# Attention with the output projection inside its loop, and a reordered stick-breaking mixer

## The chip, the cores and the metric

One core of a Trainium2 chip runs the whole program. Its engines each take their own instructions in order and meet at semaphores: TensorE (PE; PEld is its weight load), VectorE (DVE), ScalarE (ACT), GpSimd (POOL) and SyncE (SP, which issues DMAs). PSUM, where matmuls write, has 8 banks of 512 float32 values for each of 128 partitions. The metric is the device time of one execution in microseconds (us).

## What is computed

256 tokens of width 1024 pass a first block of two layers (feed-forward, mixer, feed-forward, gated embedding) and a second block of two layers (attention, then experts chosen by a top-k). The three places that matter here, cut down:

```python
# first block, layer 0: stick-breaking attention, 16 heads of 64
q, k, v = jnp.split(h @ w_qkv, 3, axis=-1)
q = rms_norm(q.reshape(B, S, 16, 64), q_gain)      # and k alike
z = jnp.einsum('bhqd,bhkd->bhqk', qb, kb) * scale
log_stay = jnp.where(causal, jax.nn.log_sigmoid(-z), 0.0)
log_after = lax.cumsum(log_stay, axis=3, reverse=True) - log_stay
weights = jnp.where(causal, jnp.exp(jax.nn.log_sigmoid(z) + log_after), 0.0)
o = einsum('bhqk,bhkd->bhqd', weights, vb);  return o @ w_o

# second block, layer 0 (MLA, keys of 128 + 64 rotated) and layer 1 (DSA), 8 heads of 128
s = einsum(q, k) * scale;  s = jnp.where(mask, s, -jnp.inf)
p = jax.nn.softmax(s, axis=-1);  o = einsum(p, v);  return o @ w_o
# in DSA the mask is a top-64 of an index score for each query
```

## The kernel before, in words

All weights come as a stream of units of 128 x 1024 float32 (512 KB). SP loads them into a ring of 6 (`raw`). `split` makes two parts of a unit: ScalarE copies it to a rounded high part (`w_hi`, ring of 4, line 655) and VectorE subtracts that to get the low part (`w_lo`, ring of 6, line 1106). ScalarE may split unit u only when unit u-4 is used. TensorE waits for the low part in `unit()` and multiplies with three matmuls per product (`mm3`, lines 1848 to 1850): high by high, high by low, low by high. `rows` multiplies the 256 tokens by 8 units into `acc(0)` (banks 0 to 3) or `acc(1)` (banks 4 to 7): 12 matmuls of 512 columns a unit.

The order on each engine is the order written in its function, and each function calls `split` at chosen places, so the place of a `split` in ScalarE's and VectorE's lists is fixed. Of the loops, only the feed-forward one is a loop on the chip; all others are written out.

**Stick-breaking mixer** (layer 0 of the first block). TensorE: q's rows into acc(0), k's into acc(1); it waits for the copy of k, transposes q (`turn_rows`, line 1880) into banks 0 to 3, multiplies v into acc(1), and behind v's sixth unit waits for k's normed rows and transposes k into banks 0 to 3. `head_norm` on VectorE squares (line 1234), reduces, waits for GpSimd's power (line 488) and multiplies (line 1242), with splits between. `keep_acc` on ScalarE (line 728) copies a product out of PSUM; `keep_turned` (line 714) copies transposes. Then `stick_breaking`: for 8 pairs of heads, TensorE's logits (lines 1982, 1983), VectorE's mask and size (1267, 1269), ScalarE's exp and log (791, 792), VectorE's stay (1274), TensorE's sums (1991, 1992), ScalarE's exp (782), TensorE's mix (2000 to 2002), ScalarE's high and VectorE's low part of the output (786, 1279). A pair uses two banks, in turn over all 8. The output projection goes into acc(0), and `late_norm` transposes x into banks 4 to 7.

**Attention** (MLA and DSA), 8 heads. A head's scores (TensorE, line 2032) go to bank n % 4; VectorE masks them (1328 in MLA, two instructions; 1331 in DSA, one) and takes the maximum (1336); ScalarE's exp (818); VectorE divides by the sum (1342, 1344); TensorE transposes the weights (2047) into bank 4 or 5; ScalarE copies them (824); TensorE mixes (2057, 2058) into bank 6 or 7; ScalarE takes the high part (810) and VectorE the low part (1248) of the head's output. Turn n of VectorE handles the mask of head n, the division of n-1 and the low part of n-3; turn n of ScalarE the exp of n, the copy of n-1 and the high part of n-2. There is no split within the loop: up to four units of the projection are split ahead of it, the rest behind. When all heads are done, `rows` runs the projection: 8 units into acc(0), and the layer norm follows. In DSA VectorE finds the top 64 in 8 rounds ahead of the attention, each with a split ahead of it, and TensorE transposes q (banks 0 to 3) and k (banks 4 to 7) behind v's rows.

Of the kernel before, what the change touches and what calls it, by code (L numbers as in the profile page):

```python
# [24 lines left out]
F32 = mybir.dt.float32  # L25
# [34 lines left out]
KEY_TURN = 5  # L60
# [47 lines left out]
KEPT_MLA = 3 + PARTS + 2  # L108
N_UNITS = sum(n for _, n in unit_plan()) + SPLIT
# [110 lines left out]
def program(nc, stream, x_in_dram, consts, stickc, poolc, scalec, ropec, lnc, subkeys, out):  # L220
    with ExitStack() as ctx:
# [166 lines left out]
        def logit(p):  # L388

            r = 2 * (p % 4)  # L390
            return ps[:, r:r + 2, 0:PAIR]

        def mixed(p):
            r = 2 * (p % 4)
            return ps[:, r:r + 2, PAIR:PAIR + P]
# [26 lines left out]
        diags, row = blk(E_DIAG, DIAG_RING, NK), blk(E_ROWS, ROW_RING, 2 * D)  # L422

# [214 lines left out]
        def _(act):  # L638
# [139 lines left out]
            def stick_breaking():  # L778
# [29 lines left out]
            def heads_high(k, bank):  # L808
                act.wait_ge(o_done, t.after(o_done))
                act.activation(act_hi[:, k, :], ps[:, bank, 0:T], ACT.Copy).then_inc(o_hi, 1)  # L810
# [92 lines left out]
            for i in range(DEPTH):  # L903
# [3 lines left out]
                if i == 0:  # L907
# [27 lines left out]
                early_norm(4 * i + 2, 1 + i)  # L935
# [11 lines left out]
            for i in range(DEPTH):  # L947
# [5 lines left out]
                if i == 0:  # L953
# [50 lines left out]
                    attention(M_SM, M_PT)  # L1004
                else:
# [25 lines left out]
                    split(KD)  # L1031
                    keep_acc(v_tok, 1)
                    keep_turned(area(A_QT, 2048), range(4))
                    keep_turned(area(A_KT, 2048), range(4, 8))
                    attention(S_SM, S_PT)
                if i == 1:
                    split(KD - SPLIT)
# [7 lines left out]
                split(KD - 1)  # L1045
# [45 lines left out]
        def _(dve):  # L1091
# [136 lines left out]
            def head_norm(rows, scale, eps):  # L1228
# [15 lines left out]
                split(KD - 5)  # L1244

            def heads_low(k, bank):
                dve.wait_ge(o_hi, t.after(o_hi))
                dve.tensor_tensor(act_lo[:, k, :], ps[:, bank, 0:T], act_hi[:, k, :].bitcast(F32),
# [12 lines left out]
            def stick_breaking():  # L1261
# [30 lines left out]
                for p in range(2, N_PAIRS):  # L1292
# [3 lines left out]
                    if p + 2 < N_PAIRS:  # L1296
                        stays(p + 2)
                output_low(N_PAIRS - 1)
# [21 lines left out]
            def attention(sm_at, mask, scale):  # L1320
                sm = blk(sm_at, H2, PAIR)
                parts = ((0, P), (P, PAIR))
                for n in range(H2 + 3):
                    if n < H2:
                        dve.wait_ge(s_done, t.after(s_done))
                        if isinstance(scale, list):
                            for b, (lo, hi) in enumerate(parts):
                                ins = dve.scalar_tensor_tensor(sm[:, n, lo:hi], ps[:, n % 4, lo:hi], scale[b],
                                                               mask[:, lo:hi], ALU.mult, ALU.add)
                        else:  # L1330
                            ins = dve.scalar_tensor_tensor(sm[:, n, :], ps[:, n % 4, 0:PAIR], scale, mask,
# [15 lines left out]
                    if n >= 3:  # L1347
                        heads_low(n - 3, 6 + (n - 3) % 2)
# [39 lines left out]
            for i in range(DEPTH):  # L1388
# [3 lines left out]
                if i == 0:  # L1392
# [3 lines left out]
                    head_norm(q_tok, 1.0, HD * EPS)  # L1396
                    head_norm(k_tok, 1.0 / HD, EPS)
# [3 lines left out]
                    for n in range(PARTS):  # L1401
                        b, c = part(n, 1)
                        dve.tensor_tensor(x[:, b, c], acc(0)[:, b, c], x[:, b, c], ALU.add).then_inc(x_ready, 1)
# [9 lines left out]
                early_norm(4 * i + 2, 1 + i)  # L1413
# [9 lines left out]
            for i in range(DEPTH):  # L1423
# [7 lines left out]
                if i == 0:  # L1431
# [40 lines left out]
                    attention(M_SM, area(M_ROPE + 128, PAIR), [small[:, 22 + b:23 + b] for b in range(TB)])  # L1472
# [1057 lines left out]
```

## Time and profile before

| | us |
|---|---|
| median of 3 runs (lowest, highest) | 2760.16 (2758.28, 2761.77) |
| the profiled execution | 2757.85 |
| its span | 2756.0 |
| TensorE busy / VectorE / ScalarE / GpSimd | 2542.8 / 2062.0 / 1279.2 / 1147.6 |
| stick-breaking mixer, q's rows to the end of its projection | 205 to 338 |
| MLA attention and its projection | 1062.6 to 1112.7 |
| DSA attention and its projection | 2024.9 to 2067.6 |
| last stage (rows gathered for the experts) | 2067.7 to 2756 |

Times of the trace count from the span's start. A row of a timeline has its start, its length, the engine, the line of the kernel, the operation, what it writes and reads, and how many like it follow one another; in brackets stands how long the engine was idle before it and whose work it waited for. `arena` is the big tile in SBUF in which nearly everything lives, `ps` is PSUM, `act_both` holds the high and low parts of the activations. The length of an instruction includes a part in which the next one already runs, so the distance of two starts is what an instruction takes in a row of such.

### The profile page before, as it was taken

The page shows a single profiled execution, that of the slowest core. Times are in us where ns is not written, and L with a number is a line of the kernel's source. Part 1 is how long each engine was busy: PE and PEld are TensorE (multiplying, and loading weights), DVE is VectorE, ACT ScalarE, POOL GpSimd, SP SyncE. Part 2 cuts the span into 40 slices and gives each one's busy share as a digit, 9 for nine tenths or more (in the row PEclk, how much of TensorE's full clock was granted, in tenths as well). Part 3 has the DMA queues.
Part 4 walks back from the last instruction along what each step waited for, and adds up shares of the span by engine and source line. Part 5 has one row for each costly group of instructions (what it writes and reads, how often), then busy time and mean ns, then how long its engine had stood idle before and what let it go on. Part 6 is the DMA issues. An engine that isn't in the chain of part 4 may idle for free.

```text
span 2756.0 us, 38867 instructions
## 1 busy us (share of the span) xinstructions
PE 2542.8 (92%) x12724; PEld 1980.0 (72%) x12724; DVE 2062.0 (75%) x4122; ACT 1279.2 (46%) x2160; POOL 1147.6 (42%) x1482
## 2 busy tenths in 40 slices
PE   8999899999999999999999899999987888887777
PEld 7887688878888877899999788887765333433223
DVE  7886588788878876798999567666777776777675
ACT  5555555555555555555555445455443222222222
POOL 4443044344434411388787533331103444444443
PEclk9999999999999999999999999999999999999998
DMA  9996799889979966455556799997938999999998
GB/s 356 379 320 211 283 384 373 279 328 377 324 264 383 368 222 218 153 175 182 183 180 198 250 382 389 383 385 285 314 129 341 422 416 422 412 422 419 414 411 341
DMA packets 217832, 873.30 MB, mean 317 GB/s; under 512 B 38320, under 2 KB 38448, under 8 KB 184048
## 3 DMA queue, kind: packets, MB, share of 16 engines
q0 software_dynamic: 118496, 511.47, 47.6%
q1 hardware_dynamic: 99072, 359.38, 37.0%
q10 hardware_dynamic: 144, 1.05, 0.1%
q8 instruction: 51, 0.84, 0.1%
q14 instruction: 69, 0.57, 0.1%
HBM read 786.70 MB, written 152.17 MB: 341 GB/s over the span
## 4 chain that ended last, share of the span: by engine, by line
PE 50%; DMA 21%; POOL 12%; DVE 7%; issue 5%; ACT 3%; SPq 0%; DVEq 0%; POOLq 0%; ACTq 0%
PE ps L1931 12%; DMA arena<-both_rows,arena 11%; POOL gate_cells L544 11%; PE ps L1848 8%; PE ps L1849 8%; PE ps L1850 8%; DMA both_rows<-in_stream 8%; PE ps L2294 6%; PE ps L1933 6%; DVE arena L1739 2%; PE ps L2251 1%; DMA raw<-in_stream 1%; DVE w_lo L1106 1%; PE ps L2032 1%; ACT w_hi L655 1%
## 5 line engine op out<-in xcount | busy, mean ns | idle before, releaser
L1106 DVE TENSOR_TENSOR w_lo<-raw,w_hi 128x1024 fp32r<-128x1024 f32 x665 | 811.0, 1223 | 290.4 <-ACT w_hi L655 285.8
L655 ACT ACTIVATE w_hi<-raw 128x1024 fp32r<-128x1024 f32 x665 | 701.8, 1058 | 461.0 <-DMA raw<-in_stream 316.3
L2294 PE MATMUL ps<-arena 128*128 128x512 f32 x1024 | 483.1, 620 | 126.5 <-ACT arena L872 126.4
L1931 PE MATMUL ps<-act_both,w_hi 128*128 128x512 f32 x1408 | 502.3, 399 | 6.6 <-DVE act_both L1134 4.8
L2294 PEld LDWEIGHTS ps<-arena 128*128 128x128 f32 x1024 | 192.8, 196 | 406.1 <-ACT arena L872 204.4
L1739 DVE SCALAR_TENSOR_TENSOR arena<-arena 128x1024 f32<-128x1024 f32 x256 | 313.6, 1225 | 186.6 <-DMA arena<-both_rows,arena 184.9
L583 POOL DMA_INDIRECT arena<-both_rows,arena x256 | 290.5, 1135 | 369.5 <-PE ps L2294 342.5
L516 POOL DMA_DIRECT2D both_rows<-arena x512 | 280.1, 554 | 353.1 <-DVE arena L1183 343.4
L1848 PE MATMUL ps<-w_hi,act_both 128*128 128x512 f32 (+1 forms) x990 | 386.0, 390 | 26.1 <-DVE w_lo L1106 12.8
L1933 PE MATMUL ps<-act_both,w_lo 128*128 128x256 f32 x1408 | 394.8, 280 | 0.0
L1849 PE MATMUL ps<-w_lo,act_both 128*128 128x512 f32 (+1 forms) x990 | 383.0, 387 | 0.0
L1850 PE MATMUL ps<-w_hi,act_both 128*128 128x512 f32 (+1 forms) x990 | 382.5, 387 | 0.0
L544 POOL DMA_INDIRECT gate_cells<-hot x256 | 316.0, 1235 | 110.2 <-issue 83.2
L1848 PE MATMUL ps<-act_both,w_hi 128*128 128x256 f32 x1192 | 339.5, 285 | 3.6 <-DVE act_both L1140 1.5
L1849 PE MATMUL ps<-act_both,w_hi 128*128 128x256 f32 x1192 | 338.0, 284 | 0.0
L1850 PE MATMUL ps<-act_both,w_lo 128*128 128x256 f32 x1192 | 337.9, 283 | 0.0
L1931 PEld LDWEIGHTS ps<-act_both,w_hi 128*128 128x128 f32 x1408 | 264.5, 188 | 74.9 <-issue 4.5
L1933 PEld LDWEIGHTS ps<-act_both,w_lo 128*128 128x128 f32 x1408 | 265.8, 189 | 3.0
L865 ACT ACTIVATE hot<-hot 128x2 f32<-128x2 f32 (+1 forms) x132 | 26.8, 203 | 458.3 <-DVE arena L1739 457.5
L1848 PEld LDWEIGHTS ps<-w_hi,act_both 128*128 128x128 f32 x990 | 188.1, 190 | 69.6 <-DVE w_lo L1106 12.0
L1848 PEld LDWEIGHTS ps<-act_both,w_hi 128*128 128x128 f32 x1192 | 229.4, 192 | 5.1 <-issue 3.8
L1849 PEld LDWEIGHTS ps<-act_both,w_hi 128*128 128x128 f32 x1192 | 229.5, 193 | 0.0
(276 smaller groups left out, 3652.8 us busy)
## 6 DMA issues: line engine op xcount, KB each, us to landing
raw<-in_stream SPq DMA_DIRECT2D x675, 512.0 KB, 3.4
arena<-in_stream POOLq DMA_DIRECT2D x128, 512.0 KB, 9.7
both_rows<-arena POOLq DMA_DIRECT2D x512, 128.0 KB, 6.3
both_rows<-in_stream POOLq DMA_DIRECT2D x128, 512.0 KB, 7.0
gate_cells<-hot POOLq DMA_DIRECT2D x32, 512.0 KB, 21.2
hot<-gate_cells POOLq DMA_DIRECT2D x128, 128.0 KB, 7.0
gate_cells<-hot POOLq DMA_INDIRECT x256
arena<-both_rows,arena POOLq DMA_INDIRECT x256, 10.8
```

What stands on the lines that cost most here:

```text
L516: pool.dma_start(rows.rearrange("(c r) k -> r c k", r=32), arena[32 * a:32 * a + 32, A_RELAY_OUT + UNIT * s:A_RELAY_OUT + UNIT * s + UNIT] ...
L544: pool.indirect_dma_start(gate_cells[:, :], bass.IndirectOffsetOnAxis(ap=cell[:, q:q + 1], axis=0), weights[:, q:q + 1], None).then_inc(sc ...
L583: pool.indirect_dma_start(row[:, p % ROW_RING, :], None, both_rows[:, :], at).then_inc(row_in[p % ROW_RING], 16)
L655: act.activation(w_hi[:, u % SPLIT, :], raw[:, u % RAW, :], ACT.Copy).then_inc(hi_done, 1)
L1106: dve.tensor_tensor(w_lo[:, u % RAW, :], raw[:, u % RAW, :], w_hi[:, u % SPLIT, :].bitcast(F32), ALU.subtract).then_inc(lo_done, 1)
L1739: dve.scalar_tensor_tensor(row[:, p % ROW_RING, 0:D], row[:, p % ROW_RING, 0:D], 1.0, x_rows[:, b, :], ALU.mult, ALU.mult, accum_out=dots[ ...
L1848: pe.matmul(dst, lhs[0], rhs[0], start=first, stop=False, **kw)
L1849: pe.matmul(dst, lhs[0], rhs[1], start=False, stop=False, **kw)
L1850: return pe.matmul(dst, lhs[1], rhs[0], start=False, stop=last, **kw)
L1931: pe.matmul(ps[:, bank, :], high, act_both[:, :, k, :], start=k == 0, stop=k == KD - 1, skip_group_check=True)
L1933: ins = pe.matmul(ps[:, bank, T:2 * T], low, act_hi[:, k, :], start=False, stop=k == KD - 1, skip_group_check=True)
L2294: ins = pe.matmul(ps[:, 2 * (n % 2) + half, :], diags[:, p % DIAG_RING, :], row[:, p % ROW_RING, D + 512 * half:D + 512 * half + 512], sta ...
```

## The change

- Stick-breaking: v's rows go to acc(0), q's banks, right behind k's rows. q is transposed behind v's second unit and k behind its seventh, both into banks 4 to 7. The pairs start at banks 4 to 7, the projection goes to acc(1), and the following norm transposes into banks 0 to 3. ScalarE copies k ahead of a split instead of behind it and v ahead of two; those two splits come within the last two turns of the loop.
- Attention: banks 0 to 3 hold the first four heads' scores and then the projection's sums; later heads' scores go to banks 4 and 5. There is one bank for transposed weights (6) and one for a head's output (7). In turn n TensorE transposes the weights of head n, multiplies unit n - lag of the projection, mixes head n and makes the scores of head n + 4; lag is 2 in MLA, 3 in DSA. `mix(n)` waits for the copy of its own weights and for the low part of head n-1. ScalarE and VectorE split one unit at the end of their turns 5 to 9 (MLA) and 3 to 10 (DSA).
- DSA: q and k are transposed behind v's third and sixth unit, both into banks 0 to 3, and the top-k has a split in the first 4 of its 8 rounds.

```diff
-KEY_TURN = 5
+QUERY_TURN, KEY_TURN = 1, 6
+SCORE_BANK, WEIGHT_BANK, MIX_BANK = (0, 1, 2, 3, 4, 5, 4, 5), 6, 7
+MLA_LAG, DSA_LAG = 2, 3
+MLA_SPLITS, DSA_SPLITS = range(5, 10), range(3, 11)
...
         def logit(p):
-            r = 2 * (p % 4)
+            r = (2 * p + 4) % 8
...
 # ScalarE
+                    else:
+                        split()
                 output_high(N_PAIRS - 1)
...
-            def attention(sm_at, pt_at):
+            def attention(sm_at, pt_at, splits):
-                for n in range(H2 + 2):
+                for n in range(H2 + 3):
...
-                        act.activation(pT[:, n - 1, :], ps[:, 4 + (n - 1) % 2, 0:PAIR], ACT.Copy).then_inc(p_kept, 1)
-                    if n >= 2:
-                        heads_high(n - 2, 6 + n % 2)
+                        act.activation(pT[:, n - 1, :], ps[:, WEIGHT_BANK, 0:PAIR], ACT.Copy).then_inc(p_kept, 1)
+                    if 2 <= n < H2 + 2:
+                        heads_high(n - 2)
+                    if n in splits:
+                        split()
...
-                    split(KD)
-                    keep_acc(k_tok, 1, roots=1)
-                    keep_turned(area(A_QT, 2048), range(4), cst[:, QG:QG + 1])
-                    split(KEY_TURN + 1)
-                    keep_turned(area(A_KT, 2048), range(4), cst[:, KG:KG + 1])
+                    split(KD - 1)
+                    keep_acc(k_tok, 1, roots=1, pending=1)
+                    split(3)
+                    keep_turned(area(A_QT, 2048), range(4, 8), cst[:, QG:QG + 1])
+                    split(KD - SPLIT)
+                    keep_turned(area(A_KT, 2048), range(4, 8), cst[:, KG:KG + 1])
                     act.preload_act_table_set("natural_log_exp_and_others")
-                    split(KD - KEY_TURN - 1)
-                    keep_acc(v_tok, 1, roots=1)
+                    keep_acc(v_tok, 0, roots=1, pending=2)
...
-                    split(KD)
-                    keep_acc(v_tok, 1)
+                    split(2)
                     keep_turned(area(A_QT, 2048), range(4))
-                    keep_turned(area(A_KT, 2048), range(4, 8))
-                    attention(S_SM, S_PT)
+                    split(2)
+                    keep_turned(area(A_KT, 2048), range(4))
+                    keep_acc(v_tok, 1, pending=SPLIT)
+                    attention(S_SM, S_PT, DSA_SPLITS)
...
 # VectorE
-                split(KD - 5)
+                split(after)
...
                     if n >= 3:
-                        heads_low(n - 3, 6 + (n - 3) % 2)
+                        heads_low(n - 3)
+                    if n in splits:
+                        split()
...
-                    head_norm(q_tok, 1.0, HD * EPS)
-                    head_norm(k_tok, 1.0 / HD, EPS)
+                    head_norm(q_tok, 1.0, HD * EPS, KD - 6)
+                    head_norm(k_tok, 1.0 / HD, EPS, 2)
...
-                        if n < KD:
+                        if n < KD - SPLIT:
                             split()
...
 # TensorE
-            def attention(sm_at, pt_at, terms, values_pending=False):
+            def attention(sm_at, pt_at, terms, lag):
+                used, ready = t.value(s_used), t.value(act_ready)
                 def scores(h):
-                    if h >= 4:
-                        pe.wait_ge(s_used, t.after(s_used))
-                    s, both = ps[:, h % 4, :], terms(h)
+                    if h >= 6:
+                        pe.wait_ge(s_used, used + h - 1)
+                    s, both = ps[:, SCORE_BANK[h], :], terms(h)
...
+                def turn_weights(h):
+                    pe.wait_ge(p_ready, t.after(p_ready))
...
+                def mix(h):
+                    pe.wait_ge(p_kept, t.after(p_kept))
+                    if h >= 1:
+                        pe.wait_ge(act_ready, ready + h)
...
+                def project(h):
+                    if h == 0:
+                        pe.wait_ge(s_used, used + 4)
+                    pe.wait_ge(act_ready, ready + h + 1)
+                    s = unit()
+                    for b in range(TB):
+                        for lo in (0, 512):
+                            ins = mm3(ps[:, 2 * b + lo // 512, :], a(h, P * b, P), w(s, lo, 512), h == 0, h == H2 - 1)
...
+                for n in range(H2 + lag):
+                    if n < H2:
+                        turn_weights(n)
+                    if n >= lag:
+                        project(n - lag)
+                    if n < H2:
+                        mix(n)
+                        if n + 4 < H2:
+                            scores(n + 4)
...
-                    rows(1, KD, fresh=False, then={KEY_TURN: turn_keys})
+                    rows(0, KD, fresh=False, then={QUERY_TURN: turn_queries, KEY_TURN: turn_keys})
                     stick_breaking()
-                    rows(0, KD, fresh=False, by_part=part_done, late=(KD - 2, KD - 1))
+                    rows(1, KD, fresh=False, by_part=part_done, late=(KD - 2, KD - 1))
...
+                    rows(1, KD, fresh=False, then={2: turn_q, 5: turn_k})
+                    pe.wait_ge(turned_kept, t.after(turned_kept, 4))
+                    attention(S_SM, S_PT, lambda h: ((kT[:, h, :], qT[:, h, :]),), DSA_LAG)
```

## Rows read from the trace of the kernel before

**Rows 1.** The page, part 1: TensorE's busy time, share of the span, instructions.
```profile
PE 2542.8 (92%) x12724; PEld 1980.0 (72%) x12724; DVE 2062.0 (75%) x4122; ACT 1279.2 (46%) x2160; POOL 1147.6 (42%) x1482
```
**Rows 2.** Busy time by stretch: us, busy (instructions) of each engine, clock, DMA.
```profile
1112.70:1125.00 12.30, 6.41 (x27) 5.72 (x28) 6.90 (x21) 8.58 (x16) 1.82 (x3) 0.63 0.37 130
2024.80:2045.70 20.90, 15.24 (x89) 11.89 (x89) 18.32 (x63) 15.49 (x50) 0.55 (x1) 1.00 0.00 0
```
**Rows 3.** Timeline of TensorE, stick-breaking: start, length, instruction, [idle before, releaser].
```profile
247.11 1.91 PE L1880 MATMUL ps<-cst,arena 128*128 128x128 f32 x16
250.48 0.50 PE L1848 MATMUL ps<-w_hi,act_both 128*128 128x512 f32 x1 [1.47 <-ACT arena L728]
...
269.05 3.34 PE L1880 MATMUL ps<-cst,arena 128*128 128x128 f32 x16 [1.95 <-DVE arena L1242]
...
278.06 0.71 PE L1982 MATMUL ps<-arena 64*128 64x256 f32 x4
...
285.03 0.91 PE L1991 MATMUL ps<-arena 128*128 128x384 f32 x2 [2.01 <-DVE arena L1274]
```
**Rows 4.** Timelines of GpSimd, VectorE and ScalarE in the same stage.
```profile
258.47 6.33 POOL L488 TENSOR_TENSOR small<-small,cst 128x32 f32<-128x32 f32 x1 [17.30 <-DVE small L1237]
...
266.71 2.28 DVE L1242 TENSOR_TENSOR arena<-arena,small 128x2048 f32<-128x2048 f32 x1
...
279.19 2.10 ACT L728 ACTIVATE arena<-ps,small 128x1024 f32<-128x1024 f32 x2
...
280.46 0.69 DVE L1267 TENSOR_TENSOR ps<-ps,arena 128x512 f32<-128x512 f32 x1
```
**Rows 5.** Timeline of TensorE, MLA attention and the start of its projection.
```profile
1073.26 0.55 PE L2047 MATMUL ps<-cst,arena 128*128 128x128 f32 x3
1073.64 0.60 PE L2057 MATMUL ps<-arena 128*128 128x256 f32 x2
...
1074.30 2.06 PE L2032 MATMUL ps<-arena 128*128 128x128 f32 x8
...
1086.43 0.55 PE L2047 MATMUL ps<-cst,arena 128*128 128x128 f32 x3 [1.70 <-DVE arena L1344]
...
1090.60 0.50 PE L1848 MATMUL ps<-w_hi,act_both 128*128 128x512 f32 x1 [0.93 <-DVE act_both L1248]
```
**Rows 6.** Timelines of ScalarE and VectorE: pieces of an attention turn, and splits.
```profile
1073.85 0.49 ACT L824 ACTIVATE arena<-ps 128x384 f32<-128x384 f32 x1 [1.01 <-PE ps L2047]
1074.50 0.39 ACT L810 ACTIVATE act_both<-ps 128x256 fp32r<-128x256 f32 x1 [0.16 <-PE ps L2058]
...
1090.13 0.42 DVE L1248 TENSOR_TENSOR act_both<-ps,act_both 128x256 fp32r<-128x256 f32 x1 [0.42 <-ACT act_both L810]
...
2048.80 1.06 ACT L655 ACTIVATE w_hi<-raw 128x1024 fp32r<-128x1024 f32 x1 [3.62 <-PE ps L1850]
2051.52 1.06 ACT L655 ACTIVATE w_hi<-raw 128x1024 fp32r<-128x1024 f32 x1 [1.66 <-PE ps L1850]
...
2049.90 1.23 DVE L1106 TENSOR_TENSOR w_lo<-raw,w_hi 128x1024 fp32r<-128x1024 f32 x1 [4.26 <-ACT w_hi L655]
```
**Rows 7.** Timelines of TensorE and then of VectorE, DSA attention.
```profile
2024.86 2.89 PE L2032 MATMUL ps<-arena 128*128 128x128 f32 x16 [1.94 <-ACT arena L714]
2029.50 0.55 PE L2047 MATMUL ps<-cst,arena 128*128 128x128 f32 x3 [1.76 <-DVE arena L1344]
...
2045.69 0.50 PE L1848 MATMUL ps<-w_hi,act_both 128*128 128x512 f32 x1 [0.93 <-DVE act_both L1248]
...
2023.47 1.23 DVE L1106 TENSOR_TENSOR w_lo<-raw,w_hi 128x1024 fp32r<-128x1024 f32 x1
...
2026.44 0.56 DVE L1331 SCALAR_TENSOR_TENSOR arena<-ps,arena 128x384 f32<-128x384 f32 x1
...
2027.56 0.55 DVE L1331 SCALAR_TENSOR_TENSOR arena<-ps,arena 128x384 f32<-128x384 f32 x1
...
2029.36 0.55 DVE L1331 SCALAR_TENSOR_TENSOR arena<-ps,arena 128x384 f32<-128x384 f32 x1
```

More of the change, by code:

```diff
@@ L1003, in _ @@
                     keep_acc(v_tok, 1)
-                    attention(M_SM, M_PT)
+                    attention(M_SM, M_PT, MLA_SPLITS)
                 else:
@@ L1044, in _ @@
                     continue
-                split(KD - 1)
+                split(KD - 1 - len(MLA_SPLITS))
                 layer_norm()
@@ L1226, in ffn, with head_norm @@
                                              ALU.add).then_inc(x_ready, 1)
-            def head_norm(rows, scale, eps):
+            def head_norm(rows, scale, eps, after):
                 dve.wait_ge(acc_kept, t.after(acc_kept))
@@ L1318, in heads_of, with attention @@
                 return tok(at, row)[:, :, off:off + h * d].rearrange("p b (h d) -> p b h d", h=h)
-            def attention(sm_at, mask, scale):
+            def attention(sm_at, mask, scale, splits):
                 sm = blk(sm_at, H2, PAIR)
@@ L1471, in _ @@
                     t.skip(acc_kept, 3)
-                    attention(M_SM, area(M_ROPE + 128, PAIR), [small[:, 22 + b:23 + b] for b in range(TB)])
+                    attention(M_SM, area(M_ROPE + 128, PAIR), [small[:, 22 + b:23 + b] for b in range(TB)],
+                              MLA_SPLITS)
                 else:
@@ L2036, in attention @@
                 for h in range(4):
                     scores(h)
-                if values_pending:
-                    pe.wait_ge(acc_kept, t.after(acc_kept))
-                for n in range(1, H2 + 2):
-                    if n <= H2:
-                        h = n - 1
-                        pe.wait_ge(p_ready, t.after(p_ready))
-                        if h >= 2:
-                            pe.wait_ge(p_kept, t.after(p_kept))
-                        for c in range(3):
-                            ins = pe.transpose(ps[:, 4 + h % 2, P * c:P * c + P],
-                                               sm[:, h, P * c:P * c + P], ident)
-                        ins.then_inc(p_turned, 1)
-                    if n >= 2:
-                        h = n - 2
-                        if h == 0 or h == H2 - 1:
-                            pe.wait_ge(p_kept, t.after(p_kept))
-                        if h >= 2:
-                            pe.wait_ge(act_ready, t.after(act_ready))
-                        o, v = ps[:, 6 + h % 2, :], slice(P * h, P * h + P)
-                        pe.matmul(o[:, 0:T], v_tok[:, 0, v], pT[:, h, 0:T], start=True, stop=False)
-                        pe.matmul(o[:, P:T], v_tok[:, 1, v], pT[:, h, T:PAIR], start=False,
-                                  stop=True).then_inc(o_done, 1)
-                    if n + 3 < H2:
-                        scores(n + 3)
@@ L2073, in _, with turn_queries @@
                 if i == 0:
+                    def turn_queries():
+                        pe.wait_ge(acc_kept, t.after(acc_kept))
+                        pe.wait_ge(rows_ready, t.after(rows_ready))
+                        turn_rows(q_tok, range(4, 8))
                     def turn_keys():
@@ L2076, in turn_keys @@
                         pe.wait_ge(turned_kept, t.after(turned_kept, 4))
-                        turn_rows(k_tok, range(4))
+                        turn_rows(k_tok, range(4, 8))
                     rows(0, KD)
@@ L2188, in terms @@
                         return (kT[:, h, :], qT[:, h, :]), (krT[r, :], qrT[r, h // 2, :])
-                    attention(M_SM, M_PT, terms, True)
+                    attention(M_SM, M_PT, terms, MLA_LAG)
                 else:
```

77 lines of the change are left out of this document (42 added, 35 removed).

## The prediction

> **What bounds the kernel now.** I read the page first: TensorE is busy 92% of the span [rows 1], so a change that only reorders work can win no more than the TensorE waits of the stages that it touches. The timeline of TensorE through each of the three stages then gives those waits, and the timelines of the other engines say who ends them.
>
> Stick-breaking stage: TensorE stands 1.47 us ahead of v's rows, until ScalarE has copied k out of PSUM, and 1.95 us ahead of the key transposes, until VectorE has multiplied k by its root [rows 3]. These 16 transposes then took 3.34 us where the same 16 took 1.91 us at 247.11 [rows 3]: the array had fallen to the lower of its two clocks (1.2 instead of 2.4 GHz). Then v's copy starts only at 279.19, behind a split on ScalarE, and the first size at 280.46, behind a split on VectorE [rows 4], and the first sums wait 2.01 us [rows 3]. From there the chain VectorE, ScalarE, VectorE sets the pace.
>
> MLA attention: TensorE has work almost without a pause; of the loop's waits only 1.70 us (weights of head 6) and 0.93 us ahead of the projection are worth a name [rows 5]. DSA attention: VectorE sets the pace, and in 20.9 us TensorE is busy 15.24 [rows 2]. It starts late because VectorE's top-k runs to 2026.44 [rows 7].
>
> **Stick-breaking.** q, k and v take the same matmuls. v goes to q's banks, so it needs neither k's copy nor q's transposes; both sets of transposes come behind v's units 1 and 6. I lay the stage out from the end of k's rows, 246.94 (0.17 ahead of the row at 247.11, as at any end of a run of matmuls here). TensorE's own work to the end of v is 8 units of 2.72 us (from ScalarE's starts at 2048.80 and 2051.52, each released by a unit [rows 6]) and two transposes of 1.72 (1.91 less the overlap with the next): 25.2, so 272.1, if nothing waits. Query transposes at 252.4: k's copy, with the split now behind it, is done at 249.4. Key transposes at 267.7: k's squares start at 249.4, split and reduction follow, GpSimd's root takes 6.33 us [rows 4] to 261.8, four splits lie beside it, the product of 2.28 us [rows 4] ends at 264.3. So there are 3 us to spare, and no fall of the clock. Before, the logits started at 278.06 [rows 3]: 5.9 us gained. The copy of v now starts at once and the first size at 273.1, since no split stands ahead of either; from there size, exp, log and stay are the same chain (280.46 to 285.03 before [rows 3, 4]), so the first sums come at 277.7 instead of 285.03. **Gain 7.4 us.** What is late next is the same VectorE and ScalarE chain, and it is not changed. The two splits put into its last two turns fall where ScalarE has no exp waiting; they delay the last output by about 1.2 us, and that is used only by the projection's eighth unit, 19 us later. The norm that moves to banks 0 to 3 costs nothing: it waits for the same x, and those banks are free by then.
>
> **The two attention loops.** Removed: the pass of 8 projection units behind the loop, 8 x 2.72 = 21.8 us, and the waits of 1.70 and 0.93 [rows 5] or 0.93 [rows 7]. Added: the same 8 units in the turns. Moved: 5 and 8 splits on ScalarE and VectorE. The number of matmuls is the same; the new order of the score matmuls I cost at nothing, between -1 and +1 us. Prefetch on SP follows the units, which are now used more slowly, so it has more time; GpSimd's load of the sub-keys, behind the last mix, has 6.6 us to land and is first read behind the layer norm, over 15 us later: nothing.
>
> What counts is a new wait. There is now one bank for a head's output, so the mix of head n waits until VectorE has taken the low part of head n-1. Follow what lies between two mixes, by start to start times. Low part to matmul 0.47 (1090.13 to 1090.60 [rows 5, 6]); mix 0.66 [rows 5]; scores 1.99 in MLA (2.06 less the overlap [rows 5]) or 0.73 in DSA (2.89 for four heads [rows 7]), while there are any (turns 0 to 3); transposes to ScalarE's copy 0.59 [rows 5, 6]; the copy 0.39 (0.49 less 0.10 overlap) and the high part 0.28 [rows 6]. Now comes the split, last in ScalarE's turn: high to low 1.10 and the low part of the weights 1.14 (1.23 less 0.09 overlap) [rows 6], and only behind it, in VectorE's next turn, mask, maximum and division, 1.80 together (the two masks at 2027.56 and 2029.36 [rows 7]), and then the low part of head n. Without scores that is 6.4 us, with them 7.15 in DSA; MLA's mask is two instructions, so I take 6.6 there. TensorE's own turn is 0.38 + 2.72 + 0.66 = 3.76, or 4.49 with scores. So every turn with a split in it leaves TensorE waiting 2.6 to 2.8 us: **the splits have been put into a ring that runs through all three engines.** Without a split the ring is 3.5 to 4 us, and TensorE hides it.
>
> MLA, scores from 1062.64 as before. Turns 0 and 1 have no projection to hide the one bank: waits of 0.75 and 1.48, mix 1 at 1076.2. Turns 2 and 3 are TensorE's own (0.38 + 2.72 + 0.66 + 1.99 = 5.75). The first split is in turn 5 of ScalarE, behind the transposes of head 4 (1090.4), so mix 4 waits: 1096.3; then mix 5 at 1102.9, mix 6 at 1108.2, mix 7 at 1112.8 (no mask any more), and two units to 1119.4. Before, 1090.60 + 21.8 = 1112.4 [rows 5]. **Loss 7.0 us.**
>
> DSA. q and k are transposed within v's rows, and 4 of the 8 splits leave the top-k, each 1.14 (one stands at 2023.47 [rows 7]): mask 0 at 2026.44 - 4.56 = 2021.9; TensorE has the scores from 2020.2, for which the two transposes fill a pause of 0.8. Transposes of head 0 at 2025.5 (3.06 behind the mask as before [rows 7], and 0.5 more for v's copy and the exp table on ScalarE). Mix 0 26.6, mix 1 29.9; turn 3 of VectorE holds the first split, so mix 2 waits 5.4 us, to 2037.0; then 2044.2, 2051.3, 2057.7, 2063.0, 2067.6, and three units to 2076.6. Before, 2045.69 + 21.8 = 2067.5 [rows 7]. **Loss 9.1 us**, although the loop starts 4.6 us earlier.
>
> Restarts: a first matmul behind a wait is 0.10 longer (0.50 against 0.40), some ten times: 1 us at most. The clock: it fell to 0.63 on average over 1112.7 to 1125, after 4.6 us without work, and stayed at 1.00 in the DSA loop with waits up to 1.9 [rows 2, 7]. The 5.4 us wait ahead of mix 2 is in the first class: I take 1.3 us for it, between 0 and 3. A page bears on this: the Trainium skill ("TensorE: Matmul & The Clock Gate", Why this matters for your kernels) says that a longer gap between bursts sends the array back to the half clock; by that rule each wait of 2.8 us might do it, which is the third rival below.
>
> Sum: -7.4 + 7.0 + 9.1 + 0.6 + 1.3 = +10.6 us. Everything behind each stage follows its end: the feed-forward stages have TensorE busy, and the last stage starts from the layer norm. The profiled execution took 2757.85 us (span 2756.0), so 2768.5; it lies 2.3 below the median of the runs shown. I say 2769.
>
> **Rivals.** (1) The ring doesn't bind, TensorE does: the split is done early because ScalarE reaches it before the transposes. Then DSA's loop is its own work, 36 us and 6 of first waits, from 2020.2 to 2062.2 (-5.4), MLA's ends at 1110.9 (-1.5), and with the stick-breaking gain the sum is -14.3: 2743.6. For it speaks that most of the work is TensorE's [rows 1]; against it that ScalarE takes its instructions in the order written, and the split stands behind the copy of the turned weights. It decides as soon as the ring is under 4.5 us. The Trainium skill has a rule against this change even then ("Perfetto Trace Analysis", Optimizing Tensor Performance): matmul groups should rotate through PSUM banks so that emptying one overlaps the next. By it alone, with the splits out of the way, one mix bank costs only the first two turns of a loop, 2 us each, which is in this rival's sum.
> (2) The ring is there but shorter, since less of each piece is exposed than start to start times say: losses of 3 and 4.5 us against the gain of 7.4: 2758.
> (3) The clock falls within the loops and stays low. TensorE's turn doubles from 4.49 to 9.0 in DSA and from 3.76 to 7.5 in MLA, over the ring: some 6 and 2 us more: 2777. For it: waits of 2.7 us in every turn; against it: 1.00 in rows 2 at 73% busy.
> (4) The stick-breaking part gives nothing, because the clock or the chain takes it back: 2776.
>
> **Chances.** Forecast 0.58 (own range 2762 to 2775), (1) 0.13, (2) 0.13, (3) 0.11, (4) 0.05. The range reaches over the forecast, (2) in its upper half, (3) and (4): 2756 to 2780, leaving out (1) and the tails. A measurement of this kernel can tell about 0.2%, 5.5 us, from no change: faster by more (under 2754.6) 0.14, within 0.14, slower by more (over 2765.7) 0.72.
>
> **What would show it.** Right: in the profile after, the mixes wait for VectorE's low part 2.6 to 2.8 us a turn in the second half of MLA's loop and all through DSA's, the longest ahead of mix 2 of DSA; VectorE's splits there wait 3 us for ScalarE's; from the first scores to the end of the projection MLA takes 56.8 us instead of 49.8 and DSA 56.4 instead of 42.6; the stick-breaking stage has no wait ahead of v and the key transposes. Wrong: loops in which TensorE has no waits after turn 2 (rival 1), or a granted clock of 0.5 through them (rival 3), or a stick-breaking gain under 5 us.

## The result, and the profile after

| | before | after |
|---|---|---|
| median of ten runs each, us | 2758.11 (2753.23 to 2762.13) | 2765.77 (2763.12 to 2769.97) |
| the profiled execution, us | 2757.85 | 2763.59 |
| its span, us | 2756.0 | 2761.8 |

The ratio is 1.0028, with a 95% interval of 1.0018 to 1.0037: 7.7 us slower. The forecast was 2769 us, in a range of 2756 to 2780.

The page's busy times hardly moved (after; compare [rows 1]):

```profile
PE 2541.1 (92%) x12724; PEld 1980.0 (72%) x12724; DVE 2059.4 (75%) x4122; ACT 1276.7 (46%) x2160; POOL 1147.4 (42%) x1482
```

TensorE is busy 1.7 us less (its busy time includes time at the lower clock) and the span is 5.8 us longer, so it waits 7.5 us more. The reader finds where by laying the same landmarks of the two TensorE timelines side by side. The x transposes that open each norm are good ones, since every kernel has them. The stages between them, in us:

| kernel | to the norm behind stick-breaking | from there to MLA's scores | MLA scores to norm | to the norm of the DSA block | from there to the norm behind DSA's attention | of it from DSA's scores | rest of the span |
|---|---|---|---|---|---|---|---|
| before | 338.1 | 724.5 | 54.6 | 800.8 | 152.7 | 45.9 | 685.3 |
| after | 330.0 | 721.7 | 59.4 | 800.2 | 165.1 | 64.3 | 685.4 |

Stick-breaking gave 8.1 us (0.7 of it was there at 199 us already, ahead of the stage), MLA's loop cost 4.8 (5.3 to the last matmul of its projection; the wait ahead of the norm is 0.5 shorter), DSA's stage 12.5. TensorE in the stick-breaking stage after (columns as in [rows 3]): no wait ahead of v or of the key transposes, 1.91 us instead of 3.34 for them, first sums at 276.95 instead of 285.03.

```profile
251.43 1.91 PE L1896 MATMUL ps<-cst,arena 128*128 128x128 f32 x16
...
266.81 1.91 PE L1896 MATMUL ps<-cst,arena 128*128 128x128 f32 x16
```

TensorE in MLA's loop after ([rows 5] before): L2049 scores, L2056 transposes of the weights, L2064 the mix. The mixes of heads 1 and 4 to 7 wait for VectorE's low part (L1260):

```profile
1051.68 6.77 PE L2049 MATMUL ps<-arena 128*128 128x128 f32 x32
...
1063.82 0.67 PE L2064 MATMUL ps<-arena 128*128 128x256 f32 x2 [1.41 <-DVE act_both L1260]
...
1074.67 0.59 PE L2064 MATMUL ps<-arena 128*128 128x256 f32 x2
...
1082.91 0.67 PE L2064 MATMUL ps<-arena 128*128 128x256 f32 x2 [2.69 <-DVE act_both L1260]
...
1089.99 0.67 PE L2064 MATMUL ps<-arena 128*128 128x256 f32 x2 [1.50 <-DVE act_both L1260]
```

And in DSA's loop after ([rows 7] before):

```profile
2018.58 1.02 PE L2064 MATMUL ps<-arena 128*128 128x256 f32 x2 [0.58 <-ACT arena L834]
...
2023.36 0.67 PE L2064 MATMUL ps<-arena 128*128 128x256 f32 x2 [1.41 <-DVE act_both L1260]
...
2030.49 1.19 PE L2064 MATMUL ps<-arena 128*128 128x256 f32 x2 [5.25 <-DVE act_both L1260]
...
2039.28 0.67 PE L2064 MATMUL ps<-arena 128*128 128x256 f32 x2 [1.57 <-DVE act_both L1260]
...
2046.42 1.19 PE L2064 MATMUL ps<-arena 128*128 128x256 f32 x2 [2.53 <-DVE act_both L1260]
...
2053.93 0.67 PE L2064 MATMUL ps<-arena 128*128 128x256 f32 x2 [2.03 <-DVE act_both L1260]
```

The length of a mix tells the clock: 0.67 us is full speed behind a wait, 0.59 without one, 1.0 to 1.2 the lower level. It tells it for that moment only: behind the mix of 0.67 us at 1082.91 the clock fell, and the granted clock of that turn was 0.76 on average. One turn of VectorE and ScalarE between the mixes at 2039.28 and 2046.42 shows the ring link by link:

```profile
2041.19 0.49 ACT L834 ACTIVATE arena<-ps 128x384 f32<-128x384 f32 x1 [2.03 <-PE ps L2056]
2041.58 0.38 ACT L820 ACTIVATE act_both<-ps 128x256 fp32r<-128x256 f32 x1
2041.84 1.06 ACT L663 ACTIVATE w_hi<-raw 128x1024 fp32r<-128x1024 f32 x1
...
2042.94 1.23 DVE L1118 TENSOR_TENSOR w_lo<-raw,w_hi 128x1024 fp32r<-128x1024 f32 x1 [3.81 <-ACT w_hi L663]
2044.08 0.55 DVE L1346 SCALAR_TENSOR_TENSOR arena<-ps,arena 128x384 f32<-128x384 f32 x1
...
2045.86 0.42 DVE L1260 TENSOR_TENSOR act_both<-ps,act_both 128x256 fp32r<-128x256 f32 x1
```

High part 2041.58, ScalarE's split 2041.84, VectorE's split 1.10 later (after 3.81 us of waiting for it), mask 1.14 later, low part 1.78 later, mix 0.56 later. The distance of the two mixes is 7.14 us; the prediction's ring had 7.15.

### The profile page after: what moved, and what is told of

The parts are those of the page before. It is cut to its first block, busy times and chain, and to the rows that moved or that the text cites. A ratio compares the mean times of both kernels' runs of the same rounds, so it can differ in the third digit from the quotient of the medians.

```text
span 2761.8 us, 38878 instructions
## 1 busy us (share of the span) xinstructions
PE 2541.1 (92%) x12724; PEld 1980.0 (72%) x12724; DVE 2059.4 (75%) x4122; ACT 1276.7 (46%) x2160; POOL 1147.4 (42%) x1482
## 4 chain that ended last, share of the span: by engine, by line
PE 47%; DMA 23%; POOL 12%; DVE 8%; issue 6%; ACT 3%; SPq 0%; DVEq 0%; POOLq 0%; ACTq 0%
DMA arena<-both_rows,arena 12%; PE ps L1947 12%; POOL gate_cells L552 11%; DMA both_rows<-in_stream 10%; PE ps L1864 7%; PE ps L1865 7%; PE ps L1866 7%; PE ps L1949 6%; PE ps L2328 5%; DVE arena L1755 2%; DVE w_lo L1118 1%; PE ps L2285 1%; DMA raw<-in_stream 1%; ACT w_hi L663 1%; PE ps L2049 1%
```

## The experiments

The times of the kernel before shift a little from one set of runs to the next, so each ratio is to the runs beside it. Theory throughout: two splits of one unit, placed in the same turn, tie low part n to low part n+1 through ScalarE. Rivals: the single mix bank alone; TensorE's own work; the clock.

**Stick-breaking alone.** Edit: the parts of the diff on q, k, v and the banks 0 to 3 of the next norm, on the kernel before; both attentions as before.

> The kernel before with the stick-breaking part alone; both attention loops as before. My theory: the whole gain of that part, 7.4 us, is kept to the end, so 2750.7 us against 2758.1 (ratio 0.9973), with 330.0 instead of 338.1 us at the x transposes behind the stage, and no stage behind it changed. In the changed kernel MLA's scores also came 3.1 us earlier than this gain explains (before, ScalarE's splits in MLA's preparation wait for weights to land). If that belongs to where the transfers fall once the stick-breaking stage is shorter, it shows here too: about 2748 us (0.996), scores at 1051.7. If it was chance, scores are at 1054.8. Rival: what the stage gains is given back downstream, ratio 1.000.

Measured: ratio 0.9982 (0.9973 to 0.9991), 5.0 us faster, the forecast of 7.4 at the edge of the interval. The stage itself is as in the changed kernel (norm behind it at 330.6), and the later stages are those of before: 54.6 and 45.9 us for the two attentions. MLA's scores came at 1053.42, between the two values named, which settled nothing yet (the next experiment and the last one settle it). The gain is kept to the end.

**Each loop alone beside it.** Edit: the changed kernel with the three `attention` functions, splits and bank numbers of before called for MLA (first) or for DSA with its order of transposes (second).

> The changed kernel with MLA's attention put back as before: stick-breaking part and DSA loop alone. My theory: the parts add. In the trace of the changed kernel the DSA stage ends 12.4 us later against the clock of its own start (-6.8 at 1911, +5.6 at the end of the projection), so -7.4 + 12.4 = +5.0: 2763.1 us (ratio 1.002). If the price of the DSA loop were only the 9.1 us of my prediction, +1.7: 2759.8 (1.0006). Rival: the loss came mostly from MLA's loop, then 2751 (0.997).

> The changed kernel with DSA's attention and the order of its q and k transposes put back as before: stick-breaking part and MLA loop alone. My theory: MLA's loop costs what its stage shows, from the first scores to the end of the projection 55.2 instead of 49.9 us, +5.3, beside -7.4 and the 3.1 us found ahead of the scores: -5.2, 2752.9 us (ratio 0.998). By my prediction's 7.0 for the loop and without the 3.1: -0.4, 2757.7 (1.000). Rival: an attention loop with the projection inside is no loss in itself, then 2748 (0.996).

Measured: with the DSA loop 1.0029 (1.0017 to 1.0041), with the MLA loop 1.0004 (0.9994 to 1.0014). The 1.002 expected of the first lies within its interval; the 0.998 expected of the second doesn't, and 1.000, the prediction's 7.0 without the 3.1 us ahead of the scores, does. Against stick-breaking alone that is +13 and +6 us; by the stages, DSA 164.7 against 151.9 (+12.8) and MLA 60.0 against 54.6 (+5.4). By the stages the costs add, 18.2 us where the changed kernel has 17.3. By the times of whole executions they add less well: 13 and 6 make 19, and the changed kernel lies 12.7 above stick-breaking alone (1.0028 against 0.9982), which the intervals of about 0.1% each just allow. Neither kernel lost anything in the stage that it has as before. From the norm behind stick-breaking to MLA's scores the first took 720.6 us, the second 723.3, with the same instructions up to there. All eleven kernels with the new stick-breaking stage, the changed one among them, lie between 720 and 724 us there, and the timelines of ScalarE differ in that stretch by what its splits wait for a weight unit to land (3.85 us once at 1052.05 in the kernel before; 3.38 us once at 1042.83 in the kernel with stick-breaking alone; 2.66 and 1.74 us in the kernel of the next experiment). The kernel before took 724.5 us there. The last kernel below is the kernel before with only its MLA score matmuls in another order, so its code is the same up to there, and it took 721.8, with waits of 2.30 and 1.45 us. So the 2.8 us that the changed kernel gained there are not its own.

**ScalarE's splits one turn earlier.** The smallest cut through the ring; bank, lags and VectorE stay.

```
-MLA_SPLITS, DSA_SPLITS = range(5, 10), range(3, 11)
+MLA_HIGH, DSA_HIGH = range(4, 9), range(2, 10)
+MLA_LOW, DSA_LOW = range(5, 10), range(3, 11)
```

> The changed kernel with ScalarE's splits one turn earlier in both loops and VectorE's where they are, so VectorE's split no longer waits for the high part of the next head. One mix bank, lags and all else stay. My theory: the ring is cut, since low part of head n, split, mask, division and low part of head n+1 (3.4 us) run beside low part, mix, scores, transposes, copy, high part (3.1 us). TensorE's own turn (5.4 and 3.8 us in MLA, 4.5 and 3.8 in DSA) then decides: MLA's waits ahead of mixes 4 to 6 go (-6 us at least), in DSA mix 2 waits under 2.5 us instead of 5.25 and the others under 0.5, the clock stays at 1.00: -14 us. Sum -18 to -24 against the changed kernel: 2742 to 2748 us (0.994 to 0.996 of the kernel before). Rival A: the single mix bank is the cause by itself, the split only fills a wait that is there anyway: the mixes still wait 2.6 us a turn, 2766 (1.003). Rival B: ScalarE's earlier splits wait for a unit that the projection has not freed or for its landing, and delay exp and copy: 2755 to 2760.

Measured: 0.9962 (0.9948 to 0.9976), 2744.09 us, 10.5 faster than before and some 18 faster than the changed kernel. MLA takes 52.1 us from scores to norm, 7.3 less than in the changed kernel, and DSA 47.6, 16.7 less (at least 6 and 14 were expected). The clock did not stay at 1.00 in the first turns: 0.76 granted behind mix 1 of MLA, 0.62 behind mixes 0 and 1 of DSA. TensorE's timeline, MLA and then DSA:

```profile
1062.82 0.84 PE L2065 MATMUL ps<-arena 128*128 128x256 f32 x2 [1.41 <-DVE act_both L1261]
...
1080.69 0.59 PE L2065 MATMUL ps<-arena 128*128 128x256 f32 x2
...
1084.44 0.59 PE L2065 MATMUL ps<-arena 128*128 128x256 f32 x2
...
2015.21 1.19 PE L2065 MATMUL ps<-arena 128*128 128x256 f32 x2 [1.40 <-DVE act_both L1261]
...
2020.15 0.67 PE L2065 MATMUL ps<-arena 128*128 128x256 f32 x2 [1.40 <-DVE act_both L1261]
...
2024.63 0.59 PE L2065 MATMUL ps<-arena 128*128 128x256 f32 x2
...
2029.00 0.59 PE L2065 MATMUL ps<-arena 128*128 128x256 f32 x2
```

Past mix 2 no mix waits, and their distances are TensorE's own 3.75 and 4.4 us. Within the loops VectorE's splits now wait at most 0.52 us for ScalarE's, instead of 2.4 to 5.9:

```profile
2028.20 1.23 DVE L1119 TENSOR_TENSOR w_lo<-raw,w_hi 128x1024 fp32r<-128x1024 f32 x1 [0.52 <-ACT w_hi L664]
```

The bank is still single, so the bank alone is not the cause; it costs the waits of 1.4 us in the turns that have no projection, and here the clock fell behind one of them. What two mix banks with the splits unmoved would give wasn't tried: all eight banks are in use.

**The splits of both engines one turn earlier, and VectorE's one turn later.** Edits: both lists `range(4, 9)` and `range(2, 10)`; or ScalarE as changed, but for its last DSA split, in turn 9 instead of 10, and VectorE `range(6, 11)` and turns 4 to 10, two in the last.

> The changed kernel with the splits of both engines one turn earlier, so that they stand to each other as in the changed kernel. My theory: what counts is that VectorE's split stands ahead of the next low part and waits for a split of ScalarE that stands behind the next high part, not how early they are. So the waits of 2.5 to 2.8 us ahead of the mixes stay and begin a turn earlier (mix 3 of MLA, mix 1 or 2 of DSA): from the scores to the next norm MLA 59 to 61 us (59.4 in the changed kernel, 52.1 with ScalarE's splits alone moved) and DSA 62 to 66 (64.3 and 47.6). Rival: an earlier split is what helped; then 52 and 48 to 50.

> The changed kernel with VectorE's splits one turn later and ScalarE's where they are. My theory: the same cut of the ring from its other side, so MLA 52 to 53 us from the scores to the next norm and DSA 47 to 50, since VectorE's split no longer waits for the next head's high part. Rival: in the kernel with ScalarE's splits moved, the help came from ScalarE's copies coming earlier behind the split; then this one stays at 57 and 60 or more.

Measured: 62.8 and 69.3 us for the first, 51.5 and 47.0 for the second (2776.03 and 2741.15 us in one run each). The first is above the 59 to 61 and 62 to 66 expected; its waits do begin a turn earlier, at mix 3 of MLA (2.69 us) and mix 1 of DSA. Earlier splits in the same relation are worse: one more turn waits, and more of them run at the lower clock. Cutting the ring from VectorE's side does as much as from ScalarE's. TensorE's timeline in DSA, of the first, with the 5.25 us twice and mixes at the lower clock, and of the second, with no wait past mix 2:

```profile
2031.19 1.19 PE L2065 MATMUL ps<-arena 128*128 128x256 f32 x2 [5.25 <-DVE act_both L1261]
...
2039.98 1.19 PE L2065 MATMUL ps<-arena 128*128 128x256 f32 x2 [5.25 <-DVE act_both L1261]
...
2020.16 0.67 PE L2063 MATMUL ps<-arena 128*128 128x256 f32 x2 [1.41 <-DVE act_both L1260]
...
2024.73 0.59 PE L2063 MATMUL ps<-arena 128*128 128x256 f32 x2
...
2029.10 0.59 PE L2063 MATMUL ps<-arena 128*128 128x256 f32 x2
```

**The projection one turn further behind.** Edit: `MLA_LAG, DSA_LAG = 3, 4`.

> The changed kernel with the projection one turn further behind in both loops (3 and 4 turns). My theory: where the ring sets the pace, a unit taken out of a turn shortens nothing, and it comes back behind the last mix, 2.72 us each. DSA: +2.7 us, the mixes at the same distances; MLA: +2.7 less the 1.1 us by which turn 2 gets shorter: +1.6. Rival (TensorE's own work is the pace): nothing changes, the unit is only done later.

Measured, in one run of 2767.97 us: 62.7 us for MLA and 65.8 for DSA, +3.3 and +1.5 where 1.6 and 2.7 were expected, together 4.8 instead of 4.3. The sum fits, the shares don't: in MLA turn 2 got a wait of 1.41 us of its own and was no shorter (mix 1 to 2 took 5.9 us, 5.5 in the changed kernel; the granted clock there was 0.71), and in DSA the time at the lower clock fell on other turns (mix 0 to 1 took 3.3 us instead of 4.8, mix 3 to 4 8.8 instead of 7.1). That TensorE's work is the pace, and the lag free, is excluded.

**A version that uses what was learned.** Scores ahead of the mix, DSA two turns behind, ScalarE's first three splits ahead of v's copy, score matmuls of odd heads in MLA reversed:

```
-                        mix(n)
                         if n + 4 < H2:
                             scores(n + 4)
+                        mix(n)
...
+    s, both = ps[:, SCORE_BANK[h], :], terms(h)[::-1] if h % 2 else terms(h)
```

> ScalarE's splits one turn earlier as before, and four things more: the scores of head n+4 ahead of the mix of head n instead of behind it, the DSA projection two turns behind instead of three, three of ScalarE's splits ahead of v's copy (so that two of VectorE's fall into its wait for the first exp), and in MLA the order of the score matmuls reversed for every odd head. My theory: the scores fill the waits ahead of mixes 0 to 2 (0.58 and 1.4 in MLA, 0.58, 1.4 and 1.4 in DSA) and projection 0 fills one more in DSA: MLA -1.5 to -2, DSA -3 to -4.5, each with less time at the lower clock. The scores of a head cost 1.99 us with contractions of 128, 64, 128, 64 rows and 1.60 with 128, 128, 64, 64; if each change between 128 and 64 rows costs 0.2, reversing every other head gives 1.40 a head, -1.6 for the eight; if the order matters for another reason, 1.60 stays. Sum against the kernel with ScalarE's splits moved: -5 to -8 us, 2736 to 2739 us, 0.993 to 0.9945 of the kernel before. Rival: VectorE becomes the pace once the waits are gone, since its turn is 3.4 to 3.7 us, and nothing more is won: 0.996.

Measured: 0.9936 (0.9921 to 0.995), median 2734.27 us of six executions. The profile is of the slowest of them, 2742.88 us; the others took 2733.25 to 2738.91. In it DSA takes 44.9 us, 2.7 less than with ScalarE's splits alone moved, a little short of the 3 to 4.5 expected, and MLA 55.2, 3.1 more. Its timeline of TensorE says where MLA's time went, and ScalarE's says what it began with:

```profile
1058.11 0.88 PE L2056 MATMUL ps<-cst,arena 128*128 128x128 f32 x3 [2.72 <-DVE arena L1360]
1058.78 3.07 PE L2049 MATMUL ps<-arena 128*128 128x128 f32 x8
...
1063.99 3.22 PE L2049 MATMUL ps<-arena 64*128 64x128 f32 x8
...
1052.40 1.06 ACT L664 ACTIVATE w_hi<-raw 128x1024 fp32r<-128x1024 f32 x1 [3.17 <-DMA raw<-in_stream]
```

Behind a wait of 2.72 us a head's scores took 3.1 and 3.2 us, where they take 1.6 at full clock; the lower level lasted until 1071.

**Two follow-ups and the score order alone.** Edits: VectorE's first two DSA splits in turns 1 and 2, without the reversed order (first) and with it (second); and the kernel before with only the order of its MLA score matmuls changed.

> The kernel with scores ahead of the mixes and DSA's lag of two, but with MLA's score matmuls in the order of the changed kernel for every head, and VectorE's first two splits in turns 1 and 2 of DSA's loop instead of both in turn 0. My theory of the earlier profile: the shorter scores left TensorE 2.72 us without work ahead of MLA's first transposes, the granted clock fell for some 14 us and took back more than it gave; and the two splits in turn 0 stood ahead of the first division, so DSA's first transposes waited 3.92 us instead of 2.58. Then here: four heads of scores take 6.77 us, MLA's first transposes wait under 1 us, scores to norm 50 to 51.5 us in MLA (55.2 there, 52.1 with ScalarE's splits alone moved), in DSA 43 to 44.5 (44.9 and 47.6). 2735 to 2739 us, 0.993 to 0.9945. Rival: the lower clock in MLA came from something else and stays, 54 us or more.

> The same with the score matmuls of every odd head of MLA reversed. DSA as in the one beside it. My theory: TensorE's work is 3.1 us shorter, but the first transposes wait for mask, maximum, exp and division of head 0, 7.6 us behind the first score, so 2 to 2.7 us of it are a wait; where the clock falls behind it, MLA takes 53 to 55 us, where it does not, 49. Between 0.5 us faster and 3 us slower than the one beside it. Rival: the saved time is kept, 1.5 us or more faster.

> The kernel before with nothing changed but the order of MLA's score matmuls: first the 128-row contraction for both column ranges, then the 64-row one, reversed for odd heads. Theory: the 32 matmuls of the first four heads take 4.9 us instead of 8.32, as in the other kernels, whatever stands around them; each later head 1.2 to 1.4 instead of 1.99. In the loop before, mask, exp and division then become the pace, so the stage (54.6 us from scores to norm) is 1 to 5 us shorter. Rival: the 4.9 needs what stands around it in the other kernel, 6.8 or more here.

Mixes 0 and 1 of MLA's loop on TensorE's timeline of the first, with no wait any more:

```profile
1059.52 0.70 PE L2064 MATMUL ps<-arena 128*128 128x256 f32 x2
...
1062.21 0.70 PE L2064 MATMUL ps<-arena 128*128 128x256 f32 x2
```

The first transposes of MLA's loop in the second:

```profile
1059.82 0.52 PE L2056 MATMUL ps<-cst,arena 128*128 128x128 f32 x3 [1.07 <-DVE arena L1360]
```

Measured: 0.9933 (0.992 to 0.9947) and 0.9928 (0.9914 to 0.9941), so the three versions can't be told apart by time. MLA took 48.2 and 47.5 us, DSA 44.6 in both, where I had 50 to 51.5 and 53 to 55 or 49 for MLA and 43 to 44.5 for DSA. The reversed order had its wait ahead of the first transposes here too, but of 1.07 us, and the clock held. The second and the version above have the same code up to the end of MLA's stage, they differ only in where VectorE's first two DSA splits stand. So the 55.2 us there are not what its edits cost: they are one execution, and the same code took 47.5 in another. What differed is when the last weight unit ahead of the loop landed: ScalarE waited 3.17 us for it there, v's copy started 2.9 us behind the first score instead of 1.2, and the wait ahead of the first transposes was 2.72 us instead of 1.07. My explanation by the shorter scores was only half of it. The score order alone gave 4.90 us for the 32 matmuls of four heads instead of 8.32, each later head 1.6 (1.2 to 1.4 expected), and 50.9 us for the stage instead of 54.6. Its single run took 2753.74 us, where nine runs of the kernel before lie between 2751.64 and 2760.09, so only the stage shows the gain.

```profile
1060.03 4.90 PE L2032 MATMUL ps<-arena 128*128 128x128 f32 x32
1066.01 0.52 PE L2047 MATMUL ps<-cst,arena 128*128 128x128 f32 x3 [1.08 <-DVE arena L1344]
```

## Why the prediction was right, and which terms were mis-sized

The direction, the mechanism and its places were right; the sum was +10.6 us, the spans gave +5.8 and the medians +7.7. That it came out this near is in part luck: two mis-sized terms nearly cancel, the score order in MLA (3.1 us too much) and the clock in DSA (2.9 too little), and weight units that landed earlier ahead of MLA hid 2.8 us in the profile.

- **Stick-breaking, -7.4.** The stage gave just that (8.12 less the 0.7 from ahead of it), by the steps named: no wait, no fall of the clock at the key transposes, copy of v and first size at once. Alone it measured 5.0, with 7.4 at the edge of the interval.
- **The ring.** By distances between mixes in DSA, forecast and measured: mix 1 to 2 7.1 and 7.13, 3 to 4 7.1 and 7.14, 5 to 6 5.3 and 5.37, 6 to 7 4.6 and 4.70. In MLA 3 to 4 8.6 and 8.24, 5 to 6 5.3 and 5.36, 6 to 7 4.6 and 4.71. VectorE's splits waited 2.4 to 5.9 us for ScalarE's, where the text said 3. The sign "2.6 to 2.8 us a turn" came true only ahead of mix 4 of each loop (2.69 and 2.53); the later mixes waited 0.7 to 2.0 us. The prediction's own distances had that for the last two (5.3 and 4.6 less a turn of 3.76), and behind a fall of the clock the projection fills more of the turn. Moving either engine's splits by one turn removed the waits, moving both did not: that is shown.
- **MLA, +7.0.** 5.3 measured to the end of the projection, which is what the 7.0 counts, and 4.8 to the norm. The mis-sized term is the order of the score matmuls, costed at nothing, between -1 and +1: 1.60 instead of 1.99 us a head, 3.1 for eight. With it the forecast would have been +3.9, and a stretch at the lower clock behind mix 4 (mix 4 to 5 took 7.08 where 6.6 was forecast) is 0.5 of the remaining 1.4. In the kernel before with nothing but its scores reordered a later head took 1.60 us too, so the saving belongs to the order and not to the loop.
- **DSA, +9.1 and most of 1.9 for clock and restarts.** 12.5 measured. From the stage's start the scores came 5.9 us earlier (4.7 forecast) and from there on the stage took 18.4 more (13.8, and 1.3 for the clock). The mis-sized term is the clock: mix 0 to 1 took 4.78 us instead of 3.3, mix 2 to 3 8.79 instead of 7.2, mix 4 to 5 7.51 instead of 6.4, 4.2 us together where 1.3 was taken. In each of these turns a mix was 1.0 to 1.2 us long. With VectorE's splits one turn later, mix 1 to 2 took 3.28 at full clock, as forecast for such a turn.
- **Ahead of MLA's scores, nothing forecast.** 2.8 us came from when weight units landed. It is no part of the change, since the kernel before and the one with only its scores reordered have the same code there and differ by as much (724.5 and 721.8), and it hid part of the loss.
- **The rivals.** (1), TensorE as the bound, is excluded for the changed kernel, and it is what the kernel becomes once the splits are a turn apart: it had 2743.6 us, 0.9948 of before, and the interval measured begins there (0.9948 to 0.9976). There the rule of the Trainium skill ("Perfetto Trace Analysis", Optimizing Tensor Performance) on rotating banks is borne out in the turns without a projection, 1.4 us each, and in no other. (2), a shorter ring, is excluded by the distances. (3) was right as a mechanism and too large: the clock fell in some of the turns and came back. The rule of the Trainium skill ("TensorE: Matmul & The Clock Gate", Why this matters for your kernels) on longer gaps between bursts agrees with the turn behind the wait of 5.25 us, with a granted clock of 0.50 in the 3 us behind it. The waits of 2.5 to 2.7 us are shorter than the gaps that this rule speaks of, and most of them had the same effect: in the changed kernel 2.53 us was followed by a slow turn, 2.69 by a half slow one, and 2.03 by none. (4) is excluded: the interval of stick-breaking alone ends at 0.9991, below no change.

## What to carry to other kernels

Work that is moved into another loop to fill it must be placed on every engine so that its second half doesn't wait for a first half of the same turn: one turn between them was worth 18 us here, and with ScalarE's splits moved no other stage got longer by more than 0.4 us. Before calling a shared buffer the cause, draw the ring of waits through all engines and name each link with its row; where its length fits the distance between two like instructions, cut the link that is cheapest to move.

## What the runs showed of the hardware

- **The order of contractions of unlike height matters.** Score matmuls of a single head over 128, 64, 128, 64 rows took 1.99 us, over 128, 128, 64, 64 rows 1.60, and the reversed order, 64, 64, 128, 128, 1.60 too. Four heads in a row took 8.32, 6.77, and with every second head reversed 4.90 us, the same matmuls each time. I had expected 0.2 us for each change between 128 and 64 rows. In the row of four the first step fits that (eight changes fewer, 1.55 us, 0.19 each), the second doesn't (three fewer, 1.87 us, 0.62 each). It comes only where a reversed head follows directly on another, so that two 64-row groups stand side by side that lie in different halves of the rows; whether that is the reason wasn't tried.
- **The clock fell behind most waits of 2.5 us and more inside a busy loop.** In the attention loops of ten kernels 20 waits of TensorE lasted 2.49 to 2.72 us; behind 17 of them the granted clock of the following 3 us was 0.50 to 0.84, behind three it was 1.00. Behind all seven of 3.92 and 5.25 us it was 0.50 to 0.59. It fell twice behind a wait of 1.41 us (the mix of 0.84 us at 1062.82 with ScalarE's splits moved, and the mix of 0.95 us at 1063.23 with the projection further behind), where ten others of 1.41 us had 1.00, and at the start of DSA's loop, where the four heads of scores stand between two pauses (mix 0 at 1.02 in the changed kernel, after waits of 2.58 and 0.58). With the projection further behind the same place held, 0.70 at mix 0. With DSA's attention as before, where these waits are 1.77 and 0.57, mix 0 took 0.60 us in the profile of the kernel before and 1.06 in two others. A turn that the clock fell in got up to 1.6 us longer, and hardly longer (6.66 instead of 6.6 us in MLA with the projection further behind) where it had a wait to spare.
- **When a weight unit lands differs from execution to execution with the same code.** ScalarE's longest wait for one in the last 30 us ahead of MLA's scores was 3.85 us in the kernel before and 2.30 in the kernel that has the same code up to there. That moved a stage by 3 us between kernels that don't differ there, and in one execution a late unit stood ahead of a fall of the clock that the same code didn't have in another (MLA 55.2 and 47.5 us).
